# Roots applied to the products of the feed-forward layers instead of to their input

## What is computed

```python
def rms_norm(x, g):
    xf = x.astype(jnp.float32)
    y = xf * lax.rsqrt(jnp.mean(xf * xf, -1, keepdims=True) + EPS)
    return (y * g.astype(jnp.float32)).astype(x.dtype)
...
def conv_ffn(x, w_up, conv_w, conv_b, w_down):
    u = x @ w_up
    s = u.shape[1]
    half = CONV_W // 2
    up = jnp.pad(u, ((0, 0), (half, half), (0, 0)))
    c = conv_b
    for j in range(CONV_W):
        c = c + conv_w[j] * up[:, j:j + s]
    g, val = c[..., :FFN_HIDDEN], c[..., FFN_HIDDEN:]
    return (jax.nn.gelu(g) * val) @ w_down
...
        h = h + rms_norm(a, norm_g[i, 1])
        f = conv_ffn(rms_norm(h, norm_g[i, 2]), ffn_w_up[i], ffn_conv_w[i], ffn_conv_b[i], ffn_w_down[i])
        h = h + rms_norm(f, norm_g[i, 3])
```

## Time and profile before

| | us |
|---|---|
| median of 3 runs | 1057.07 (1056.88 to 1058.06) |
| the profiled execution | 1056.94 |
| its span in the profile | 1055.1 |

### The profile page before, as it was taken

How to read it: one execution, slowest core, us unless ns; L and a number is a source line. 1 busy time by engine, 2 the same in 40 slices (tenths; PEclk the granted TensorE clock), 3 DMA queues, 4 the chain that set the end, 5 groups by cost and what they waited for, 6 DMA issues and landing times.

```text
span 1055.1 us, 21644 instructions
## 1 busy us (share of the span) xinstructions
PE 1026.9 (97%) x8138; PEld 941.0 (89%) x8138; DVE 667.6 (63%) x1094; ACT 557.1 (53%) x1014; POOL 418.1 (40%) x283
## 2 busy tenths in 40 slices
PE   9999999999999999999999999999999999999997
PEld 7788699999978888699999987899999999999996
DVE  4555867767767766777676766766676555554445
ACT  5655665555564654665555556644543455554442
POOL 1000243334333443433343363865653375533331
PEclk9999999999999999999999999999999999999999
DMA  9334456566434443365655624333213245446551
GB/s 354 102 120 140 159 182 206 188 201 191 151 138 160 156 135 128 124 210 184 201 191 167 205 77 160 104 119 120 81 62 121 81 140 157 151 135 215 195 181 42
DMA packets 46284, 161.82 MB, mean 153 GB/s; under 512 B 5264, under 2 KB 6544, under 8 KB 46096
## 3 DMA queue, kind: packets, MB, share of 16 engines
q1 hardware_dynamic: 45072, 156.79, 44.7%
q0 software_dynamic: 1152, 4.19, 1.2%
HBM read 159.91 MB, written 1.05 MB: 153 GB/s over the span
## 4 chain that ended last, share of the span: by engine, by line
PE 89%; DVE 5%; ACT 2%; POOL 2%; issue 1%; DMA 0%; DVEq 0%; SPq 0%; ACTq 0%
PE work L411 13%; PE work L413 13%; PE work L412 13%; PE work L1849 9%; PE acc L411 6%; PE acc L412 6%; PE acc L413 6%; PE work L2567 4%; PE work L2579 3%; PE acc L2579 2%; PE acc L2096 1%; PE acc L2110 1%; PE acc L2112 1%; PE acc L1941 1%; PE work L1387 1%
## 5 line engine op out<-in xcount | busy, mean ns | idle before, releaser
L380 POOL TENSOR_TENSOR low<-raw,high 128x1024 fp32r<-128x1024 f32 x110 | 269.0, 2449 | 276.5 <-ACT high L367 274.0
L380 DVE TENSOR_TENSOR low<-raw,high 128x1024 fp32r<-128x1024 f32 (+1 forms) x185 | 271.0, 1473 | 147.9 <-ACT high L367 147.8
L367 ACT ACTIVATE high<-raw 128x1024 fp32r<-128x1024 f32 (+2 forms) x295 | 298.6, 1026 | 36.6 <-DMA raw<-in_w_out 23.7
L411 PE MATMUL work<-xh,high 128*128 128x256 f32 (+1 forms) x1032 | 290.0, 281 | 2.1 <-DVE v_sb L1534 1.7
L412 PE MATMUL work<-xl,high 128*128 128x256 f32 (+1 forms) x1032 | 287.9, 279 | 0.0
L413 PE MATMUL work<-xh,low 128*128 128x256 f32 (+1 forms) x1032 | 287.8, 279 | 0.0
L411 PEld LDWEIGHTS work<-xh,high 128*128 128x128 f32 (+1 forms) x1032 | 193.2, 187 | 9.0 <-issue 5.6
L412 PEld LDWEIGHTS work<-xl,high 128*128 128x128 f32 (+1 forms) x1032 | 193.3, 187 | 1.7
L413 PEld LDWEIGHTS work<-xh,low 128*128 128x128 f32 (+1 forms) x1032 | 193.3, 187 | 0.2
L1290 POOL TENSOR_TENSOR h<-gelu,cv 128x256 f32<-128x256 f32 x44 | 49.7, 1130 | 194.3 <-ACT gelu L1214 87.6
L1849 PE MATMUL work<-xh,high 128*128 128x256 f32 x256 | 76.7, 300 | 0.0
(11 more groups left out here) (402 smaller groups left out, 2172.5 us busy)
## 6 DMA issues: line engine op xcount, KB each, us to landing
raw<-in_w_ffn SPq DMA_DIRECT2D x130, 512.0 KB, 4.3
raw<-in_w_out SPq DMA_DIRECT2D x39, 512.0 KB, 4.3
raw<-in_w_att SPq DMA_DIRECT2D x32, 512.0 KB, 3.9
...
```

Source lines behind the costliest of these rows:

```text
L367: act.activation(high[k][:, 0:w], raw[k][:, 0:w], ACT.Copy).then_inc(high_done[k], 1)
L380: eng.tensor_tensor(low[k][:, 0:w], raw[k][:, 0:w], high[k][:, 0:w], ALU.subtract).then_inc(low_done[k], 1)
L411: pe.matmul(out, lhs[0], rhs[0], start=start, stop=False)
```

## The change

Boundaries 0 and 2 take the form of boundary 1: PE transposes `hid` itself (`raw_pe`, two spins ahead and one behind), the gain of each channel is multiplied in the split (`pre_split_act`, `pre_split_dve`, eight pieces of 128x256 each), and the roots become the row `factor`. In the feed-forward layers each of the four products of a step is multiplied by `factor` in its place in PSUM, on DVE (`scaled`, L1238 of the kernel after), ahead of ACT's middle tap, which now waits for it. DVE's order in a step becomes: `scaled` 0, low 5 of the step before, taps 0, `scaled` 1, low 0, taps 1, low 1, `scaled` 2, low 4, taps 2, `scaled` 3, low 2, taps 3. Step 1 is written out ahead of the loop. Boundary 3 multiplies `hid` by a diagonal matrix of the roots on PE instead of transposing `hn`, with six spins ahead for seven and none behind. Gains arrive as columns of `vec`, so three loads of `pre_gain` (512 KB each, POOL's queue) go; a pad keeps the later buffers at the same places modulo 256 bytes. In `post_dve` the order of the additions moves by one. The products of the gates go to `acc[0:16, 0]` instead of `W[2]`.

```diff
+    pad(160)
...
+    def split_seen(n):
+        return 4 + KB * (n - 1)
+    HN_SEEN = {n: 4 * (n - 1) for n in range(1, 5)}
...
     def pre_pe(pe, n):
         pe.wait_ge(g["const"], 48)
-        spin(pe, W[3][:], 7)
-        for t in range(NT):
-            for half in range(2):
-                pe.wait_ge(n_["hn"], 4 * (n - 1) + 2 * t + half + 1)
-                for b in range(4):
-                    at = (4 * half + b) * P
-                    last = pe.transpose(work[:, 2 * t + half, b * P:(b + 1) * P], hn[:, t, at:at + P], ident)
+        spin(pe, W[3][:], 6)
+        for half in range(2):
+            for t in range(NT):
+                pe.wait_ge(n_["hn"], HN_SEEN[n] + t + 1)
+                for b in range(4 * half, 4 * half + 4):
+                    last = pe.matmul(raw_turned(b)[:, t * P:(t + 1) * P], hid[:, t, b * P:(b + 1) * P], diag[t],
+                                     start=True, stop=True)
                 last.then_inc(n_["turned"], 1)
-        spin(pe, acc[:, 3, :], 1)
...
-    def pre_norm(dve, n, t, half):
+    diag = [hn[:, t, 0:P] for t in range(NT)]
+    def pre_diag(dve, n, t):
         dve.wait_ge(n_["root"], 2 * n + t + 1)
-        if t == 0 and half == 0:
-            dve.wait_ge(n_["gain"], 16 * (n if n < RAW else n - 1))
-        c = cols(half)
-        dve.scalar_tensor_tensor(hn[:, t, c], hid[:, t, c], stat[:, 8 + t:9 + t], pre_gain[:, c], ALU.mult,
-                                 ALU.mult).then_inc(n_["hn"], 1)
-    RAW = 2
-    def raw_pe(pe):
+        dve.tensor_scalar(diag[t], ident, stat[:, 8 + t:9 + t], None, ALU.mult).then_inc(n_["hn"], 1)
+    RAW = (1, 2, 3)
...
+    RAW_SPINS = {1: (2, 0, 1), 2: (0, 2, 1), 3: (2, 0, 1)}
+    def raw_pe(pe, n):
+        ahead, between, behind = RAW_SPINS[n]
+        if ahead:
+            pe.wait_ge(g["const"], 48)
+            spin(pe, W[3][:], ahead)
...
+    def pre_split_act(act, n, half):
+        act.wait_ge(n_["turned"], 4 * n + (2 + half + 1 if n in RAW else 2 * half + 2))
         for b in range(4 * half, 4 * half + 4):
-            ins = act.activation(xh[:, b, :], raw_turned(b), ACT.Copy, scale=vcol("diff_gain", b, 1))
-            if b % 2:
-                ins.then_inc(n_["xh"], 1)
-    def raw_split_dve(dve):
+            act.activation(xh[:, b, :], raw_turned(b), ACT.Copy, scale=turned_gain(n, b)).then_inc(n_["xh"], 1)
+    def pre_split_dve(dve, n):
         for b in range(KB):
             if b % 2 == 0:
-                dve.wait_ge(n_["xh"], 4 * RAW + b // 2 + 1)
-            ins = dve.scalar_tensor_tensor(xl[:, b, :], raw_turned(b), vcol("diff_gain", b, 1), xh[:, b, :], ALU.mult,
-                                           ALU.subtract)
-            if b % 2:
-                ins.then_inc(n_["xl"], 1)
...
         post_mean(dve, n, 1)
+        post_add(dve, n, 0, 1)
         post_gained(dve, n, 1, 0, p, k)
-        post_add(dve, n, 0, 1)
         post_add(dve, n, 1, 0)
-        if n < 4:
+        if n == 3:
             pre_mean(dve, n + 1, 0)
         post_add(dve, n, 1, 1)
+        if n < 3:
+            pre_mean(dve, n + 1, 0)
 
     def pre_act(act, n):
...
-        if n in (0, RAW):
-            pool.wait_ge(n_["hn"], 4 * n + 4)
-            pool.dma_start(pre_gain[:], dram["pre_gain"][1 if n == 0 else 2]).then_inc(n_["gain"], 16)
 
...
                 if not (isinstance(i, int) and i + done == 0):
-                    pe.wait_ge(f[j]["g_tap"] if gate else f[j]["v_tap"], 2 * (i + done))
+                    pe.wait_ge(f[j]["g_tap"] if gate else f[j]["v_tap"], 3 * (i + done))
                 first = isinstance(i, int) and i == 0 and j == 0 and gate
...
+        up(0, 0)
+        factor_pe(pe, 2 * layer + 1)
+        up(1, 0)
         step(1)
         with pe.Fori(2, FFN_STEPS - 1) as r:
...
                 bank, s = 2 * j + value, f[j]
-                act.wait_ge(used[bank], p.base[bank] + i + 1)
+                act.wait_ge((s["g_tap"], s["v_tap"])[value], 3 * (i + done) + 1)
                 if value and not (isinstance(i, int) and i + done == 0):
...
-                    refill(split, p, bank, i)
+        def scaled(j, value, i):
+            bank, tap = 2 * j + value, (f[j]["g_tap"], f[j]["v_tap"])[value]
+            dve.wait_ge(used[bank], p.base[bank] + i + 1)
+            dve.tensor_tensor(W[bank][:, 0:TOK], W[bank][:, 0:TOK], factor, ALU.mult).then_inc(tap, 1)
+        def tapped(j, value, i):
+            bank, s = 2 * j + value, f[j]
+            mid, tap, c = (s["g_mid"], s["v_mid"])[value], (s["g_tap"], s["v_tap"])[value], (cg, cv)[value][j]
+            dve.wait_ge(mid, i + done + 1)
+            dve.scalar_tensor_tensor(c[:, 1:TOK], W[bank][:, 0:TOK - 1], ffn_taps(layer, i, j, value, 0, 0),
+                                     c[:, 1:TOK], ALU.mult, ALU.add).then_inc(tap, 1)
+            dve.wait_ge(tap, 3 * (i + done) + 2)
+            dve.scalar_tensor_tensor(c[:, 0:TOK - 1], W[bank][:, 1:TOK], ffn_taps(layer, i, j, value, 2, 0),
+                                     c[:, 0:TOK - 1], ALU.mult, ALU.add).then_inc(tap, 1)
 
         def step(i):
-            block(0, i)
-            if is0(i):
-                if layer == 0:
-                    split(p, 5, 0)
-            elif not (is_last(i) and layer == 0):
+            scaled(0, 0, i)
+            if not is0(i) and not (isinstance(i, int) and i == 1):
+                refill(split, p, 5, i - 2)
+            tapped(0, 0, i)
+            scaled(0, 1, i)
+            refill(split, p, 0, i)
+            tapped(0, 1, i)
+            refill(split, p, 1, i)
+            if is0(i) and layer == 0:
+                split(p, 5, 0)
+            scaled(1, 0, i)
+            if not is0(i) and not (is_last(i) and layer == 0):
                 refill(split, p, 4, i - 1)
-            block(1, i)
-            if not is0(i) and not (is_last(i) and layer == 0):
-                refill(split, p, 5, i - 1)
+            tapped(1, 0, i)
+            scaled(1, 1, i)
+            if not is_last(i):
+                refill(split, p, 2, i)
+            tapped(1, 1, i)
+            if not is_last(i):
+                refill(split, p, 3, i)
             if is_last(i):
+                if layer:
+                    refill(split, p, 5, i - 1)
                 for bank in (2, 3):
                     refill(split, p, bank, i)
 
+        factor_dve(dve, 2 * layer + 1)
         step(0)
-        with dve.Fori(1, FFN_STEPS - 1) as r:
+        step(1)
+        with dve.Fori(2, FFN_STEPS - 1) as r:
             step(dve.snap(r))
         step(FFN_STEPS - 1)
 
...
         for b in range(KB):
-            if b % 4 == 0:
-                pe.wait_ge(n_["xl"], 4 * 4 + 2 + b // 2)
-            last = mm3(pe, W[2][0:16, 0:TOK], wslot(4, b * 16, (b + 1) * 16), (xh[:, b, :], xl[:, b, :]), b == 0, b == KB - 1)
+            if b % 2 == 0:
+                pe.wait_ge(n_["xl"], split_seen(4) + b + 2)
+            last = mm3(pe, acc[0:16, 0, 0:TOK], wslot(4, b * 16, (b + 1) * 16), (xh[:, b, :], xl[:, b, :]), b == 0, b == KB - 1)
         last.then_inc(used[4], 1)
...
         mla_pe(pe)
-        pre_pe(pe, 1)
+        raw_pe(pe, 1)
         ffn_pe(pe, 0)
-        raw_pe(pe)
+        raw_pe(pe, 2)
         diff_pe(pe)
-        pre_pe(pe, 3)
+        raw_pe(pe, 3)
```

More of the change, by code:

```diff
@@ L550, in pre_square @@
                            accum_out=stat[:, 16 + 2 * t + half:17 + 2 * t + half]).then_inc(n_["sq"], 1)
-    def pre_split_act(act, n, t):
-        for half in range(2):
-            act.wait_ge(n_["turned"], 4 * n + 2 * t + half + 1)
-            act.activation(x_part(xh, t, half), turned(t, half), ACT.Copy).then_inc(n_["xh"], 1)
     def pre_mean(dve, n, t):
@@ L1162, in step @@
                 up(j, i)
[L1163 to L1164 removed]
+                down(j, i - 1)
         def end_by_tile(i):
```

122 lines of the change are left out of this document (51 added, 71 removed).

## The result

The kernel after takes 1069.65 us (median of 4 runs, 1068.68 to 1070.27), the kernel before 1057.11 in the same comparison: a ratio of 1.0116, 95% interval 1.0099 to 1.0134. The profiled execution took 1068.68 us. The forecast was 1068.6.

What follows compares the result with a forecast made beforehand. PE bounds the kernel before, with the DVE-ACT-POOL loop only 0.28 us a step shorter; the change makes that loop bind. Layer 0 +7.0 and layer 1 +4.7 make +11.7 on 1056.94: 1068.6 us, 8-in-10 range 1060 to 1076.

Steps and rivals of the forecast that it cites:

- The loop: Feed-forward DVE-ACT-POOL round: two value products in line add 0.66 us, from 16.41 to 17.07, over PE's 16.69.
- Layer 0: First feed-forward layer: late start, eight longer rounds and end, less reserve, make it end 7.0 us later.
- The tail: From a layer's last low 3 to its last `h`, products stand in line: +1.6 us in layer 0, +1.3 in layer 1.
- the reserve: At each layer's end, time `hl` could come later without delaying PE: 1.5 us in layer 0, 2.4 in layer 1.
- Layer 1: Second feed-forward layer: start +2.0, rounds +3.8, end +1.3, less 2.4 of reserve, make it end 4.7 us later.
- The rest: Boundaries 1 and 3, removed gain loads, earlier weight loads, gates' other bank, shifted buffers: 0, within 0.3 us.
- PE's waits: PE idle in step 1 and the last steps of each layer: 9.9 us in layer 0, 7.6 in layer 1.
- Low 5 one place later: DVE's order in a feed-forward step: moving low 5 costs nothing, since it still waits for ACT's high 5.
- Case B: Feed-forward loop has room, round stays under 16.69 us, boundary gains count: 1051.1, or 1053.5 with step 1 waits; chance 0.12.
- Case C: Feed-forward loop runs just under PE; step 1 and layer ends give back the 5.8 us: 1055 to 1059; chance 0.04.
- Case D: All four products lengthen the feed-forward loop, +1.32 us a round: about 1079 us; chance 0.09.
- Case E: Clock halves after PE's wait at layer 1's end, slowing following matmuls, +2.7 to +5.4 us: 1071 to 1074; chance 0.09.

Runs made afterwards that it cites:

- run 6: The kernel after with low 5 moved back to its old place at the end of a step: 1093.55 us, ratio 1.0338 to the kernel before.
- run 5: The kernel after with one wait more, POOL's low 3 waiting until DVE's low 5 is done: 1056.93 us, ratio 0.9992 to the kernel before.

## Why the prediction was right

**The loop.** Forecast: 17.07 us a round, for the products in line only. Measured: 17.06 in layer 0 and 17.14 in layer 1. Shown from both sides: cutting the two in line takes the loss away, cutting the other two does not, adding two in line to the kernel before makes 8 of the 12.5 us, and moving the two into the wait gives 16.40. In layer 1 the start value was too low: the loop's own round there is 16.47, not 16.41.

**Layer 0.** Forecast +7.0, measured +6.2, counted from the spins. PE's first product was forecast 3.6 us earlier and came 3.6 earlier (6.81 us behind the first spin for 10.41); the wait in step 1 at 1.8 and was 1.75. The second low 3 was forecast +1.6 and came +1.3 (156.03 - 155.14 + 0.37). Eight rounds: forecast +5.3, measured (292.56 - 286.40) - (156.03 - 155.14) = +5.3. The tail, 305.06 - 292.56 = 12.50 for 11.47, is +1.0 and not +1.6: the term that was over-sized most. Of the reserve, 1.3 was used up for a forecast of 1.5 (from the last `h` to the end it is 7.65 us for 8.97), so +1.3 + 5.3 + 1.0 - 1.3 = +6.2 within rounding.

**Layer 1.** Forecast +4.7, measured +5.4. Last low 3: 622.99 - 610.57 - 5.87 = +6.6 for a forecast of +5.8 (rounds of 17.14, and a start of +2.2 for +2.0); the tail +0.8 for +1.3. The reserve was 2.0 and not 2.4: from `h` to the first use of the last `hl` it is 640.52 - 638.05 = 2.47 us for 629.28 - 624.85 = 4.43. So rounds and start came 0.7 us over their forecast and the reserve 0.4 under, against a tail 0.5 shorter.

**The rest.** Forecast 0 within 0.3, measured +0.6. It was not taken apart by a run.

**Sum.** -0.4 (ahead of the change) + 6.2 + 5.4 + 0.6 = 11.8 for 11.7. That the sum is closer than its terms is luck: layer 0 came 0.8 us under its forecast and layer 1 0.7 over it. The profiled execution is also the shortest of the four; by the medians the loss is 12.5 us, 0.8 over the forecast.

**PE's waits** were forecast with the ends of the layers: 9.9 us in layer 0 and 7.6 in layer 1. The windows from the first product of each layer to its end show PE idle for 6.6 us (186.90 busy of 193.46, 119.25 to 312.71) and 4.9 (187.92 of 192.79, 449.67 to 642.46). Layer 0 is still 9.8 us longer from first product to end (193.46 for 183.62), as the forecast's sum has it; the other 3.3 us are busy time of PE, the factor matmuls and products at the lower clock among it. That the clock took part of this time was not in the forecast.

**Low 5 one place later** was costed at nothing, rightly, with half of the reason: the place also covers ACT's `cg`, which is worth another 1.05 us a round (1.38 - 0.33, run 6).

**Case B was priced wrongly.** The prediction gave 1051 to 1053.5 for a loop with room. A run in that state (all four cut) took 1057.93. The failing step is "the boundaries count": the loop does not start with PE but with the factor. In that run the second low 3 comes 42.3 us behind the first spin (155.74 - 113.45), as in the kernel before (155.14 - 112.81), and layer 0 takes 194.3 us from the first spin (113.45 to 307.70) for 194.0 before. PE's 2.9 us come out only where the loop is shorter by more than that, as with low 3 on DVE.

**Case C** did not occur: the round was over PE's. **Case D, all four in the loop,** did not occur either: the gate products ended before ACT's high was there, as argued. **Case E's fall of the clock did occur,** and its price did not: the prediction put matmuls at half speed on the path, while the path was the last `hh`. The Trainium skill (TensorE: Matmul & The Clock Gate, "What's actually happening") says that the clock halves after idling and returns after work; the windows above agree for two waits, with 0.66 and 0.57 on average behind 1.75 and 3.8 us, and show no fall behind two others of 1.62 and 1.77 us. Where PE does bind (run 5) such a fall stands on PE's path; what it cost there was not measured apart.

**The two lows.** The Trainium skill (SBUF — State Buffer, "SBUF: two separate sides") says that a DVE operation with two SBUF inputs and a GpSimd operation shut each other out for their whole length. The runs agree: whichever starts second is stretched, low 5 to 3.27 us, low 0 to 2.38 when POOL comes first there, POOL's `h` to 1.59 behind DVE's low 3. The products with one operand in PSUM kept their 0.42 us: the one at 181.15 in the kernel after takes 0.43 us beside POOL's `h` (180.19 to 181.84).
